# Both heads of a pair per token tile, with half of the gate and projection matmuls between the steps of the attention

## What is computed

```python
q_nope, q_rope = q[..., :A_NOPE], rope(q[..., A_NOPE:], pos)      # 128 and 64 wide
s = jnp.einsum('bhqd,bhkd->bhqk', qn, k_nope) + jnp.einsum('bhqd,bkd->bhqk', qr, k_r)
p = jax.nn.softmax(s.astype(jnp.float32) * scale, axis=-1).astype(v.dtype)
o = jnp.einsum('bhqk,bhkd->bhqd', p, v)
...
y_m = mlstm_branch(...) @ w_m_proj[l]
y_a = mla_branch(...) @ w_a_proj[l]
gates = jax.nn.sigmoid(gate_pre.astype(jnp.float32)).astype(h.dtype)
mixed = gates[..., :D_MODEL] * y_m + gates[..., D_MODEL:] * y_a
h = h + mixed @ w_out[l]
h = h + moe(rms_norm(h, norm_ffn[l]), ...)      # 32 experts, all weights are read
```

## Time and profile before

| | |
|---|---|
| median of 3 runs | 2019.34 us (2018.67 to 2023.5) |
| the profiled execution, device time | 2019.71 us |
| its span, first to last instruction | 2017.6 us |
| PE busy | 1919.4 us, 95% |
| attention, four pairs | 380.26 to 597.94 us |
| gates and projections | 597.94 to 817.70 us |

### The profile page before, as it was taken

The page is one execution under the profiler, slowest core; times in us unless marked ns, Lnnn a source line. Parts: engine busy times, 40 slices in busy tenths (PEclk is TensorE's granted clock), DMA queues, the critical chain, the costliest instruction groups (busy, mean ns, idle before and its releaser), DMA issues.

```text
span 2017.6 us, 37197 instructions
## 1 busy us (share of the span) xinstructions
PE 1919.4 (95%) x15825; PEld 896.7 (44%) x15825; DVE 423.5 (21%) x894; ACT 263.3 (13%) x563; POOL 350.4 (17%) x391
## 2 busy tenths in 40 slices
PE   7899999799999999987999999999999999999994
PEld 5356655444444444442444444444444444343432
DVE  2524534433330000252111010101010101010101
ACT  2202212122220000100101010110101010101001
POOL 3000000000003000023122213131313131313113
PEclk7899999899999999987999999999999999999997
DMA  3222211000214222426999999999999999999975
GB/s 117 86 63 63 63 42 34 13 13 0 61 43 130 75 73 62 198 114 247 396 403 403 402 402 400 405 399 406 399 407 398 408 398 407 398 407 398 407 294 184
DMA packets 153381, 485.04 MB, mean 240 GB/s; under 512 B 14048, under 2 KB 78720, under 8 KB 120528
## 3 DMA queue, kind: packets, MB, share of 16 engines
q1 hardware_dynamic: 102496, 436.66, 54.5%
q0 software_dynamic: 21552, 32.99, 6.9%
q10 hardware_dynamic: 29296, 14.86, 2.7%
HBM read 464.67 MB, written 19.96 MB: 240 GB/s over the span
## 4 chain that ended last, share of the span: by engine, by line
PE 94%; DVE 2%; DMA 2%; issue 1%; POOL 1%; ACT 0%; SPq 0%; POOLq 0%; DVEq 0%
PE PS L364 35%; PE PS L1548 33%; PE PS L1560 16%; PE PS L1449 3%; PE PS L1532 1%; PE PS L1541 1%; PE PS L1525 1%; DMA ring<-in_w_in 1%; PE PS L1328 1%; PE PS L1429 1%; PE PS L1488 1%; DMA x_sb<-acc_dram 0%; PE PS L1318 0%; DMA acc_dram<-hm_sb,ints 0%; DVE at_sb L1100 0%
## 5 line engine op out<-in xcount | busy, mean ns | idle before, releaser
L1548 PE MATMUL PS<-ring,mix_sb 128*32 128x512 f32 x6144 | 673.2, 594 | 0.0
L1548 PEld LDWEIGHTS PS<-ring,mix_sb 128*32 128x32 f32 x6144 | 196.9, 110 | 434.2 <-issue 428.7
L1560 PE MATMUL PS<-ring,hm_sb 128*32 128x256 f32 x6144 | 337.4, 379 | 0.9 <-ACT hm_sb L829 0.9
L364 PE MATMUL PS<-uT_sb,ring 128*128 128x512 f32 (+1 forms) x736 | 293.2, 554 | 6.4 <-DMA ring<-in_w_in 3.6
L1560 PEld LDWEIGHTS PS<-ring,hm_sb 128*32 128x32 f32 x6144 | 199.6, 110 | 146.0 <-issue 18.5
L1236 DVE TENSOR_SCALAR hm_sb<-PS 128x768 f32<-128x768 f32 x32 | 30.6, 958 | 917.3 <-PE PS L1548 917.3
L364 PEld LDWEIGHTS PS<-uT_sb,ring 128*128 128x128 f32 x736 | 137.9, 206 | 157.2 <-issue 157.2
L620 POOL DMA_INDIRECT acc_dram<-hm_sb,ints x96 | 151.7, 1580 | 46.8 <-POOL ints L638 24.5
L364 PE MATMUL PS<-ring 128*128 128x129 f32 (+4 forms) x592 | 147.9, 381 | 12.2 <-DVE ring L1031 5.4
L638 POOL COPY ints<-ints 128x3 int32 (+1 forms) x32 | 6.0, 187 | 723.0 <-ACT hm_sb L840 723.0
L364 PEld LDWEIGHTS PS<-ring 128*128 128x128 f32 (+1 forms) x592 | 84.3, 196 | 72.9 <-issue 50.6
(11 more groups left out here) (249 smaller groups left out, 1118.2 us busy)
## 6 DMA issues: line engine op xcount, KB each, us to landing
ring<-in_w SPq DMA_DIRECT2D x384, 1024.0 KB, 8.4
ring<-in_w_in SPq DMA_DIRECT2D x8, 1024.0 KB, 5.3
ring<-in_w_in ACTq DMA_DIRECT2D x14, 512.0 KB, 3.9
ring<-in_w_in SPq DMA_DIRECT2D x10, 512.0 KB, 5.2
ring<-m_dram POOLq DMA_DIRECT2D x16, 256.0 KB, 4.4
ring<-in_w_out SPq DMA_DIRECT2D x1, 4096.0 KB, 15.5
ring<-in_w_m_proj ACTq DMA_DIRECT2D x7, 512.0 KB, 3.7
ring<-in_w_a_proj ACTq DMA_DIRECT2D x7, 512.0 KB, 3.7
```

What stands on the lines that cost most here:

```text
L364: last = nc.tensor.matmul(out, w, r, start=n == 0, stop=n == len(pairs) - 1)
L1548: last = nc.tensor.matmul(PS[32 * j:32 * j + 32, t, :].rearrange("p (c n) -> p c n", c=2), xgT[n][:, k, 32 * t:32 * t + 32], w1_c[k][:, :, ...
L1560: last = nc.tensor.matmul(PS[32 * j:32 * j + 32, 3 + t, 0:QR], actT[:, k, 32 * t:32 * t + 32], w2_c[k // 2][:, k % 2, j * QR:(j + 1) * QR] ...
```

## The change

- The scores of both heads are made for one token tile m at a time: `qn` by `kn` for head 0 and head 1, then `qr` by `krT` alternating between the heads, whose rows are 0 to 63 and 64 to 127. The 528 keys are cut into two halves of 264, one per bank, so head 0 has banks 0 and 1 and head 1 banks 2 and 3. For one transpose to turn the meta columns of both heads, head 1 has its keys in another order (meta first); DVE makes `krT` in two halves for it, with two operations more, and a small `ckv_meta` with two more. `pr` holds four tiles, `prT` two heads.
- Between the steps PE takes four of the 16 groups "`w_in` by `uT`" and "`w_m_proj` by `hmT`" per pair (`fill`), whole or in halves, all into bank 7: gate 0 ahead of the scores, projection 0 in halves after tiles 0 and 1, gate 1 in halves after tiles 2 and 3, projection 1 ahead of the outputs. The outputs go to banks 4 and 5. The sigmoid there is an exponential on ACT (`gate_exp`), and an addition and a reciprocal on DVE (`gate_root`), the product is `gate_mix`.
- The stage after it keeps 16 groups, "`w_in` by `uT`" and "`w_a_proj` by `attT`", and adds into `mixT`. Its weights and those of `fill` are loaded by SP (`load_gates`), no longer by ACT.
- The first pair's q projections (`att_start(0)`) stand ahead of the last `turn_h`. The rotary table is loaded a second time (`rope_q`), since `mixT` is written earlier over the first.

```diff
+    ckv_meta = col(3 * META)
...
+    pr = view(ring, slot(3) + (MT + 1) * 2 * ADV, 4, TK)
+    prT = [view(ring, slot(5) + n * (MT + 1) * T, MT + 1, T) for n in range(2)]
...
+    rope_q = view(ring, slot(8), 2, T)
...
+    w_f = [[view(ring, slot(9 + p) + n * KT * P, KT, P) for n in range(2)] for p in range(2)]
...
+        def load_gates(par, n, src, at, j):
+            sp.dma_start(w_f[par][n], src[:, :, bass.ds(j * P + at, P)]).then_inc(gx_w[2 * par + n], 16)
         load_at(0, False)
+        sp.wait_ge(decay_ready, 2 * PAIRS)
+        sp.dma_start(rope_q, c_rope[:, :, 0:T]).then_inc(rope_in, 16)
+        sp.wait_ge(pe_pv, 2 * PAIRS)
+        for par in range(2):
+            load_gates(par, 0, win, C_G, par)
+            load_gates(par, 1, wmp, 0, par)
         with sp.Fori(1, PAIRS) as i:
             load_at(i, True)
...
+            for par in range(2):
+                for n in range(2):
+                    sp.wait_ge(pe_g, i * 4 + (2 * par + n - 3))
+                    passed(sp)
+                    load_gates(par, n, (win, wmp)[n], (C_G, 0)[n], i * 2 + par)
+        for par in range(2):
+            for n in range(2):
+                sp.wait_ge(pe_g, 4 * PAIRS + 2 * par + n - 3)
+                load_gates(par, n, (win, wap)[n], (C_G + D, 0)[n], par)
         sp.wait_ge(ao_ready, H + 1)
...
+            def gate_exp(par):
+                act.wait_ge(pe_g, i * 4 + (2 * par + 1))
+                act.wait_ge(mix_ready, i * 2 + (par + 1))
+                nc.scalar.activation(sg[:, par, :], bank(7), ACT.Exp, scale=-1.0).then_inc(gexp_ready, 1)
+            def turned_p(m):
+                for hh in range(2):
+                    act.wait_ge(pe_pt, i * 8 + (2 * m + hh + 1))
+                    nc.scalar.copy(prT[hh][:, 0:MT, m * P:(m + 1) * P], bank(4 + hh).rearrange("p (a b) -> p a b", a=MT)).then_inc(ptx_ready, 1)
+            gate_exp(0)
+            for m in range(MT):
+                for hh in range(2):
+                    n = 2 * m + hh
...
+                if m >= 1:
+                    turned_p(m - 1)
+            gate_exp(1)
+            turned_p(MT - 1)
...
+        for c, c1, w, a, b in ((0, META, T, bank(1), bank(2)), (T, 0, META, PS[:, 5, 32:48], PS[:, 5, 48:64])):
+            st.did(nc.vector.tensor_tensor(root[:, 2 * T:2 * T + w], a, cos[:, c:c + w], ALU.mult))
             st.alone(nc.vector.tensor_tensor(root[:, 0:w], b, sin[:, c:c + w], ALU.mult))
-            st.alone(nc.vector.tensor_tensor(krT[:, c:c + w], krT[:, c:c + w], root[:, 0:w], ALU.add))
+            st.did(nc.vector.tensor_tensor(krT[0:ROPE, c:c + w], root[0:ROPE, 2 * T:2 * T + w], root[0:ROPE, 0:w], ALU.add))
...
+            dve.wait_ge(rope_in, 32)
...
+            def gate_root(par, c0, c1):
+                if c0 == 0:
+                    dve.wait_ge(gexp_ready, i * 2 + (par + 1))
+                    st.alone(nc.vector.tensor_scalar(sg[:, par, :], sg[:, par, :], 1.0, None, ALU.add))
+                st.did(nc.vector.reciprocal(sg[:, par, c0:c1], sg[:, par, c0:c1]))
+            def gate_mix(par):
+                dve.wait_ge(pe_g, i * 4 + (2 * par + 2))
+                st.settle()
+                nc.vector.tensor_tensor(mixT[:, bass.ds(i * 2 + par, 1), :], bank(7).unsqueeze(1), sg[:, par:par + 1, :], ALU.mult).then_inc(mix_ready, 1)
+            for m in range(MT):
+                if m == 2:
+                    gate_mix(0)
+                for hh in range(2):
+                    n = 2 * m + hh
                     dve.wait_ge(pe_sc, i * 8 + (n + 1))
+                    st.alone(nc.vector.tensor_reduce(neg_max[:, n:n + 1], PS[:, 2 * hh:2 * hh + 2, 0:HALF], AX.XY, ALU.max))
...
+                for hh in range(2):
+                    n = 2 * m + hh
...
+                if m < 2:
+                    gate_root(0, m * T // 2, (m + 1) * T // 2)
+            dve.wait_ge(pe_pt, i * 8 + 8)
+            nc.vector.tensor_copy(prT[0][0:2 * META, MT, :], PS[0:2 * META, 6, :]).then_inc(ptm_ready, 1)
+            gate_root(1, 0, T)
+            gate_mix(1)
...
+        def att_start(i):
+            pe.wait_ge(at_w, i * 80 + 80)
             pe.wait_ge(ao_ready, i * 2 + 1)
...
+            pe.wait_ge(swap_ready, i * 4 + 4)
             group(pe, bank(3), [(w_swap[:, k], cqT[:, k, :]) for k in range(2)]).then_inc(pe_aq, 1)
+        def fill(i, par, n, k0, k1):
+            if k0 == 0:
+                pe.wait_ge(gx_w[2 * par + n], i * 16 + 16)
+                if n == 0:
+                    pe.wait_ge(mix_ready, i * 2 + (par + 1))
+                else:
+                    pe.wait_ge(gexp_ready, i * 2 + (par + 1))
+            src = (uT[:, :, 0:T], hmT)[n]
+            for k in range(k0, k1):
+                last = nc.tensor.matmul(bank(7), w_f[par][n][:, k], src[:, k, :], start=k == 0, stop=k == KT - 1)
+            if k1 == KT:
+                last.then_inc(pe_g, 1)
+        def att_pair(i):
+            wv = w_kv.rearrange("p (h c) -> p h c", h=2)[:, :, NOPE:NOPE + ADV]
...
+            for hh in range(2):
+                group(pe, PS[0:2 * META, 6, 256 + hh * ADV:256 + (hh + 1) * ADV], [(ckv_meta[:, (1 - hh) * META:(3 - hh) * META], wv[:, hh, :])])
...
+            fill(i, 0, 0, 0, KT)
...
+            def turn_p(m):
+                pe.wait_ge(p_ready, i * 8 + (2 * m + 2))
+                if m >= 1:
+                    pe.wait_ge(ptx_ready, i * 8 + 2 * m)
+                pair = pr[:, 2 * (m % 2):2 * (m % 2) + 2, :].rearrange("p a b -> p (a b)")
+                for hh in range(2):
+                    for j in range(MT):
+                        at = hh * (TK + META) + j * P
+                        last = nc.tensor.transpose(PS[:, 4 + hh, j * P:(j + 1) * P], pair[:, at:at + P], ident)
                     if hh == 1:
+                        last = nc.tensor.transpose(PS[0:2 * META, 6, m * P:(m + 1) * P], pair[:, T:TK + META], ident)
+                    last.then_inc(pe_pt, 1)
+            for m in range(MT):
+                if m >= 1:
+                    pe.wait_ge(exp_ready, i * 8 + 2 * m)
+                for hh in range(2):
+                    for c in range(2):
+                        nc.tensor.matmul(PS[:, 2 * hh + c, 0:HALF], qn[:, hh, m * P:(m + 1) * P], kn[:, hh, c * HALF:(c + 1) * HALF], start=True, stop=False)
+                for c in range(2):
+                    for hh in range(2):
+                        h0 = ROPE * hh
+                        last = nc.tensor.matmul(PS[:, 2 * hh + c, 0:HALF], qr[h0:h0 + ROPE, m * P:(m + 1) * P], krT[h0:h0 + ROPE, c * HALF:(c + 1) * HALF], start=False, stop=True)
+                        if c == 1:
+                            last.then_inc(pe_sc, 1)
+                if m >= 1:
+                    turn_p(m - 1)
+                fill(i, m // 2, 1 - m // 2, (m % 2) * 4, (m % 2) * 4 + 4)
+            turn_p(MT - 1)
+            fill(i, 1, 1, 0, KT)
+            for hh in range(2):
+                pe.wait_ge(ptx_ready, i * 8 + (7 + hh))
+                pe.wait_ge(ptm_ready, i + 1)
...
+                group(pe, bank(4 + hh), vs).then_inc(pe_ao, 1)
+        pe.wait_ge(pv_used, 2 * PAIRS - 1)
+        att_start(0)
+        turn_h(PAIRS - 1)
+        pe.wait_ge(t_used, H + 1)
+        att_pair(0)
+        with pe.Fori(1, PAIRS) as i:
+            att_start(i)
+            att_pair(i)
+        with pe.Fori(0, KT // 2) as i:
+            for par in range(2):
+                for n in range(2):
+                    pe.wait_ge(gx_w[2 * par + n], i * 16 + (16 * PAIRS + 16))
+                    if n == 0:
+                        pe.wait_ge(mix_ready, i * 2 + (KT + par))
+                    else:
+                        pe.wait_ge(ao_ready, H + 1)
+                    src = (uT[:, :, 0:T], attT)[n]
+                    group(pe, bank(2 * par + n), [(w_f[par][n][:, k], src[:, k, :]) for k in range(KT)]).then_inc(pe_g, 1)
...
```

More of the change, by code:

```diff
@@ L751, in _ @@
             for hh in range(2):
-                nc.scalar.copy(kn[:, hh, 0:T], bank(4 + hh)).then_inc(ak_ready, 1)
-            for n in range(2 * MT + 2):
-                if n < 2 * MT:
-                    act.wait_ge(max_ready, i * 8 + (n + 1))
-                    if n >= 3:
-                        act.wait_ge(pe_pt, i * 8 + (n - 2))
-                    s2 = PS[:, 2 * (n % 2):2 * (n % 2) + 2, :].rearrange("p a b -> p (a b)")[:, 0:TK]
-                    nc.scalar.activation(pr[:, n % 3, :], s2, ACT.Exp, bias=neg_max[:, n:n + 1], scale=(NOPE + ROPE) ** -0.5,
-                                         accum_out=row_sum[:, n:n + 1]).then_inc(exp_ready, 1)
-                if n > 1:
-                    k, m = n - 2, (n - 2) % MT
-                    act.wait_ge(pe_pt, i * 8 + (k + 1))
-                    if m == 0 and k:
-                        act.wait_ge(pe_ao, i * 2 + 1)
-                    nc.scalar.copy(prT[:, 0:MT, m * P:(m + 1) * P], bank(4 + k % 2).rearrange("p (a b) -> p a b", a=MT)).then_inc(ptx_ready, 1)
@@ L767, in _ @@
-            act.wait_ge(pe_ao, i * 2 + 2)
-        def gates(j, more):
```

(44 more changed lines are left out.)

128 lines of the change are left out of this document (44 added, 84 removed).

## The result

The kernel after takes 1944.59 us (median of 4 runs, 1941.03 to 1947.48), the kernel before 2019.36 us in the runs beside it: 0.9625 of the time, with an interval of 0.9601 to 0.9649. Five later runs, beside two of the experiments, gave 1946.57 us and 0.9652 (0.9639 to 0.9665). The forecast was 1952 us with a range from 1944 to 1970. The direction and the mechanism were right. The gain was larger than forecast, 3.75% for 3.3%, and the time that the first ratio gives, 1943.6 us, lies just outside the low end; both medians lie just inside it.

What follows compares the result with a forecast made beforehand. The prediction took PE to bound the attention pairs and gates, with the experts' weight stream issued after them. Savings of 39.5, 1.6, 11.2, 1.0, 6.6 and 7.5 sum to 67.4 us, from 2019.3 to 1952 us, range 1944 to 1970.

Steps and rivals of the forecast that it cites:

- Scores: Attention pairs: scores of a tile of both heads take 2.99 us against 2 x 2.73, saving 39.5 us in 16 tiles.
- The rule against it: Score matmuls of 264 columns: each 128-row one shows its weight load, 12.8 us less gained; as rival 1965 us, chance 0.04.
- Waits within a pair: Attention pairs: PE's waits for DVE, ACT and v get covered, gaining 2.8 us per pair, 11.2 us in all.
- The 0.2 us for bank 7: Behind gate 1 in a pair: its exponential uses the shared bank 7, so a PE wait of 0.2 us may show.
- The second rival: Attention pairs: DVE's and ACT's steps come late, PE waits about 0.9 us four times a pair; 1966 us, chance 0.12.
- Transposes and v: Attention pairs: nine transposes per tile instead of ten, v costs the same rows; about 0.4 us per pair, 1.6 in all.
- Between the stages: From attention to the remaining gates: the wait for the last attT copy has a gate group ahead, saving 1.0 us.
- the way in: Ahead of the first attention pair: the first q projections move into PE's idle time, saving 6.6 us.
- The clock: Ends of attention pairs: low clock behind waits there goes with them, saving 7.5 us, bounds 0 and 10.1.
- two bounds, 4.8 + 2.7: Low end of the range, 1944 us: changes between row counts free (4.8), low clock at the start gone too (2.7).
- Costed at nothing: DVE's added operations on krT and ckv_meta (about 1.2 us delay, covered by a 3.63 us weight wait) and SP's loads.

Runs made afterwards that it cites:

- The two experiments on the row halves: Kernel after with 64-row score matmuls ordered head by head: 1944.78 us; kernel after with head 1's reading rows 0 to 63 as head 0's do: 1960.34 us.
- late-start experiment: Kernel after with the first pair's q projections put back behind the last turn of h and its gating: 1952.76 us, 0.9671.
- the second profile: Kernel after, unchanged, run once more beside two other experiments: 1946.57 us, 0.9652.
- split-only kernel: Kernel before with only its scores cut into two halves of 264 keys, 128-row matmuls first, one head at a time, no fill: 1991.21 us, 0.9862.
- the kernel with the later wait: Kernel after with the wait for the copy to attT moved behind the next pair's q projections: 1942.10 us, 0.9629.

## Why the forecast was right, and where it was short

**Scores, right.** Forecast 2.99 us per tile and 39.5 in all; measured 2.97 and, against the 2.73 us per step of the earlier trace rows, 39.8. But in the kernel before only a step that follows other scores takes 2.73 to 2.76; the five of eight that follow transposes take 2.66, so the true gain is 4 x 9.64 = 38.6. Both prices hold apart: the eight 128-row rows take 1.88 (forecast 1.81 and 0.1 for the change), the eight 64-row ones 1.09 (1.08). The two experiments on the row halves show why.

**The rule against it, not borne out.** The 128-row rows of 264 columns, all on the same rows of the array, take 1.88 / 8 = 0.235 us each with the change included; a visible weight load of 0.1 us each would have made it 2.7 us per tile. By the rule of the Trainium skill, TensorE: Matmul & The Clock Gate, section Part 3: Packing small matmuls, those loads would have been seen; the measurement speaks against it for these fp32 rows, and decides. In a pair PEld was busy for 34.02 us beside 64.50 of PE, in 65.37.

**Waits within a pair, right in every place.** Forecast 2.8 us less per pair, measured 3.91 - 0.87 = 3.04. The 0.2 us for bank 7 did not show. The chain could be read off DVE's timeline of the kernel after, behind the scores that end at 457.88:

```profile
457.98 0.71 DVE L1131 TENSOR_REDUCE small<-PS 128x1 f32<-128x528 f32 x1 [8.82 <-PE PS L1489]
...
460.57 0.17 DVE L1136 RECIPROCAL small<-small 128x1 f32<-128x1 f32 x1
460.77 0.49 DVE L1137 TENSOR_SCALAR ring<-ring,small 128x528 f32<-128x528 f32 x1
```

The second sum is in by 460.57, 2.7 us behind the scores (forecast 2.8), the scaling ends at 461.26, 3.4 behind (3.6). PE starts its next scores at 461.41. The second rival, handovers that show, is out.

**Transposes and v, under-sized.** Everything in a pair that is neither scores nor wait gave 14.0 - 9.95 - 3.04 = 1.0 us; the forecast had 0.4. In four pairs 4.0 for 1.6, and 5.3 with the scores at 38.6. The timelines of the two third pairs say where: the transposes take 5.3 us before (five sets of 0.60, and three of 0.76 with a wait behind them) and 4.1 after, 1.2 less. v, costed at nothing, takes 2.70 before (500.70 to 503.40) and 2.39 after (511.03 to 513.42), 0.3 less. The four groups take 27.64 us and not 27.48, which gives back 0.16.

**Between the stages and the way in.** 0.95 for 1.0. The way in takes 13.70 us with the 6.87 of the q projections in it, against 14.27 without: 7.4 for 6.6. The late-start experiment bears it out (7.2).

**The clock, right in size, unproven in reason.** The first pair holds 60.19 - (65.37 - 6.87) = 1.7 us over the clean one, where the four of before held 10.1: 8.4 for 7.5. In the second profile it holds 61.43 - 58.50 = 2.9, which makes 7.2, so 7.5 was as good as the executions allow. I had said that the low clock belongs to the waits at the ends of pairs and goes with them. But in the split-only kernel those waits stayed and 5.9 of the 7.4 us at the ends of pairs went all the same, and in the kernel before the third pair has the same waits as the others and a clock of 1.00. So the waits alone don't decide where the clock falls. What does, these runs leave open.

**The range, the step that failed.** The sum for this part is 72.8 against 67.4: nearly every term came out a little above its forecast. "Transposes and v" is the one that was mis-sized most, 4.0 for 1.6. The others add 0.3 (scores), 1.0 (waits), 0.8 (way in) and 0.9 (clock, -0.3 by the second profile). I took the low end from two bounds, 4.8 + 2.7, and of those the first did not come about and the second by at most 1.0 us. Transposes, way in and waits had no bound on that side.

The second part of the failure is a term that I left out, that of the clock in the parts that the change does not touch: 3.35 + 1.29 = 4.6 us in the first profile and 1.6 in the second. Here are the first 50 us of the kernels before and after (the clock stands behind the five busy times), 0.76 and 0.83, while PE's program is the same there; in the kernel with the later wait, again the same program, it was 1.00:

```profile
0.00:50.00 50.00, 36.04 (x132) 26.79 (x133) 11.98 (x22) 9.97 (x16) 16.46 (x37) 0.76 0.37 118
```
```profile
0.00:50.00 50.00, 36.12 (x134) 27.02 (x135) 12.94 (x24) 10.93 (x16) 16.61 (x37) 0.83 0.37 118
```

The start of `att_start(0)` moved between 360.59 and 365.76 us over seven executions of kernels with the same code ahead of it. That spread of 5 us belongs in every range for this kernel; half of it below the low end would have put that near 1941. How near the miss is to chance the second measurement says: its ratio, 0.9652, is 1949 us of the same kernel before, inside the range.

**Costed at nothing, right.** The added work on `krT` did not show. The row of the kernel after that answers to the first of the earlier trace rows waits 2.53 us for the weights, where it waited 3.63:

```profile
88.67 18.03 PE L368 MATMUL PS<-uT_sb,ring 128*128 128x512 f32 x48 [2.53 <-DMA ring<-in_w_in]
```

SP's transfers were never what PE waited for in a pair.

## What to carry to other kernels

Where an engine waits on a chain of two others at each step, measure that chain from the step's end (here 2.7 and 3.4 us) and put independent work of just over that length between the steps; here it hid every wait at once, and an experiment that thins the work shows how much cover is left. Where a product's contraction is half the array's height, put a second such product on the other rows: here the two cost what one did (1.09 us for the rows of two heads or of one). And give every small term of a sum a bound of its own, and the untouched parts their spread from run to run.
